# Filter and scan of a recurrent branch on PSUM banks, with another order of steps, and another start of a streamed two-block kernel

## The chip, the cores and the metric

One core of a Trainium2 chip runs the kernel; it has a matmul engine (TensorE, PE in the profile), VectorE (DVE), ScalarE (ACT), GpSimd (POOL) and SyncE (SP), an on-chip memory SBUF and the eight PSUM banks into which TensorE writes. The metric is the device time of one launch in microseconds, lower is better. TensorE's granted clock has two levels, 2.4 GHz (1.00 in the profile) and 1.2 GHz (0.50).

## The reference

Two blocks in float32, on 512 tokens of width 1024 and, in the first block, 256 context tokens more (768 in all). Cut to what matters here:

```python
# first block: adaLN, then a mixer whose projections pass a short filter
sh1, sc1, g1, sh2, sc2, g2 = adaln(c, ada_w[layer], ada_b[layer])
h_lat = modulate(rms_norm(x, norm_mix_g[layer]), sh1, sc1)
# second block, two layers: the recurrent branch of its mixer, 4 heads of 256
xc = causal_depthwise_conv(x_r, rc_w, RNN_CONV_K) + rc_b          # 4 taps
gates = jax.nn.sigmoid(einsum('bshi,ghij->gbshj', xh, rg_w) + rg_b)
log_a = -LRU_C * gate_rec * jax.nn.softplus(-a_param)
a = jnp.exp(log_a)
mult = jnp.sqrt(-jnp.expm1(2.0 * log_a))                           # 1 at the first token
h = associative_scan(a, x * gate_in * mult)                        # h_t = a_t h_(t-1) + b_t
y_b = (h * jax.nn.gelu(y_r)) @ w_out_rnn
g_a, g_b = jnp.split(jax.nn.sigmoid(g_logits + b_merge), 2, axis=-1)
out = (g_a * y_a + g_b * y_b) @ w_o
```

## The kernel before, in words

**The stream.** All projections but adaLN's read weights as 543 chunks of 512 KB (8 tiles of 128x128). SP loads a chunk into one of two `raw` slots; ACT makes its high part `w_hi` (L987), POOL the rest `w_lo` (L415), each in four slots; TensorE makes 16 products with the high part (L442, L443, with the two parts of the activations) and 8 with the low part (L447). `chunk` (L432) is one such step. ACT makes a high part when it reaches `done()` in its own stream, so it does so between its other steps.

**The start.** Six parts of adaLN are summed up on TensorE from 48 rows of `ada_w` (`part_chunk`, L451); the 16 rows of parts 0 and 1 come in eight 1 MB loads on SP (`load_first`). A part lies in one bank as four strips of two rows, at partitions 0, 32, 64 and 96: DVE copies the bank to `arow` (`part_rows`, L1393), TensorE turns it with eight small float32 products (`turn_part`, L466), DVE adds the bias. x comes in eight loads of 384 KB on ACT's queue. ACT squares x (L1006), DVE adds the squares (L1391), two products with ones (L480, L481) sum them over the partitions; then the root, the scaling of x (L1409), parts 0 and 1, and h1, one k-tile at a time (L1428). TensorE's order: 10 rows of `ada_w`, the two ones products, `turn_part(0)`, 6 rows, `turn_part(1)`; then the projections as "items" of one chunk for 768 or 512 tokens. Item 0 (k of head 0) waits for h1 k by k, item 1 (rk) follows, item 2 (k of head 1) begins when ACT has read item 0's banks (L1044, L1045). DVE filters item 0 (L1448, L1450); products with ones for its norm stand behind item 2 on TensorE (L523, L524). Parts 2 to 5 are turned behind items 6, 13, 20 and 27.

**The recurrent branch**, two times (one per layer). TensorE makes per head h two chunks of x_r (into banks 0 and 1), the gate chunk of head h-1 (`head_gates`, banks 4 to 7) and two chunks of y_r (banks 2 and 3): five chunks a head. ACT copies x_r from the bank to a padded row in SBUF (`rows`, L1281); DVE filters it there (L1883, three times L1885) to xc, whose high part ACT makes (L1286) and whose low part DVE (L1893). After the gate chunk ACT takes four sigmoids (L1304, L1305) and exp and tanh (L1311, L1312); DVE multiplies (L1900), squares (L1903), combines (L1906); ACT takes the root (L1318); DVE sets the first token to 1 (L1912), multiplies (L1913), scans (L1914), multiplies by gelu(y_r) (L1917) and makes the low part (L1923), ACT the high part (L1291). All of head h-1 lies inside the period of head h, in both engines' order. `head_gates(h)` on TensorE waits for head h-1's sigmoids (`s_sig`).

**Behind it** come for m = 0 to 7 `conv_gates(m)` (three chunks: the convolution branch's product and two gates, in banks 0, 1, 3 for even m, 4, 5, 7 for odd m) and `rnn_product(m)` (bank 2 or 6). TensorE's order: `conv_gates(0)` (which waits for the last x_r copy and for gelu of y_r of head 3, L1298), `head_gates(3)`, a wait for its sigmoids, `conv_gates(1)`, `conv_gates(2)`, then the products. ACT takes the gates' sigmoids in pairs (`gate_pair`, L1333), DVE multiplies the first by the bank (`gated_conv`, L1860).

DVE's ops that add a product to an SBUF row elsewhere are L1787 and L1827.

## Time and profile before

| | |
|---|---|
| median of 3 runs | 3640.2 us (3639.19 to 3641.14) |
| profiled execution, its own time | 3641.35 us |
| its span | 3639.5 us, 45258 instructions |
| granted TensorE clock, mean | 0.973 |
| busy: PE, PEld, DVE, ACT, POOL | 94%, 78%, 39%, 38%, 36% |
| chain that ended last | PE 61%, issue 27%, POOL 5%, DVE 4%, ACT 3% |

The sum of a prediction for one execution goes against 3641.35 us, of which 1.85 us lie around the span. A row of the timeline groups like instructions that follow each other closely; the bracket at its end is the engine's idle time before it and what ended it.

### The profile page before, as it was taken

How to read it: one execution, taken by the hardware profiler on the slowest of the kernel's cores; microseconds unless marked ns; L12 is line 12 of the kernel's file. 1: busy time of each engine (PE TensorE's matmuls, PEld its weight loads, DVE VectorE, ACT ScalarE, POOL GpSimd, SP SyncE). 2: the span in 40 equal slices, each digit the busy share in tenths (PEclk: the TensorE clock that was granted, in tenths of full speed). 3: DMA queues.
4: the chain of work that ended last, by engine and by line, in shares of the span. 5: the costliest groups of instructions: out<-in, count | busy, mean ns of one | idle time of the engine just before them, and what ended most of it. 6: DMA issues, size and time to landing. Idle time of an engine off the chain costs nothing.

```text
span 3639.5 us, 45258 instructions
## 1 busy us (share of the span) xinstructions
PE 3425.6 (94%) x16376; PEld 2829.5 (78%) x16376; DVE 1404.4 (39%) x1696; ACT 1369.6 (38%) x1812; POOL 1310.6 (36%) x547
## 2 busy tenths in 40 slices
PE   5999899899998999899799999989998989989997
PEld 4777799778887888788687888778887867878885
DVE  5753555532204220656415321142207473262214
ACT  3434344544414441325523443244323264234423
POOL 1232000044443444344344444334443433434443
PEclk7999999999999999999899999999999999999998
DMA  6342000122222222232232223222222222223222
GB/s 236 115 140 80 2 1 1 36 92 98 98 94 80 98 98 95 79 99 87 81 99 87 87 97 98 82 92 97 94 98 81 98 76 93 93 71 108 93 98 87
DMA packets 89456, 322.08 MB, mean 88 GB/s; under 512 B 9712, under 2 KB 10096, under 8 KB 89200
## 3 DMA queue, kind: packets, MB, share of 16 engines
q1 hardware_dynamic: 87136, 315.07, 25.9%
q10 hardware_dynamic: 2192, 5.24, 0.4%
q8 instruction: 88, 1.44, 0.2%
q14 instruction: 40, 0.33, 0.0%
HBM read 318.18 MB, written 2.10 MB: 88 GB/s over the span
## 4 chain that ended last, share of the span: by engine, by line
PE 61%; issue 27%; POOL 5%; DVE 4%; ACT 3%; POOLq 0%; DMA 0%; DVEq 0%; ACTq 0%; SPq 0%
PE ps L442 14%; PE ps L443 14%; PE ps L447 14%; POOL w_lo L415 5%; PE ps L762 5%; PE ps L839 4%; PE ps L835 4%; PE ps L836 4%; DVE mt L1906 1%; PE ps L862 1%; PE ps L861 1%; PE ps L860 1%; ACT w_hi L987 1%; DVE tmp L1885 0%; DVE X L1756 0%
## 5 line engine op out<-in xcount | busy, mean ns | idle before, releaser
L415 POOL TENSOR_TENSOR w_lo<-raw,w_hi 128x1024 fp32r<-128x1024 f32 x543 | 1310.4, 2414 | 2309.8 <-ACT w_hi L987 2309.6
L987 ACT ACTIVATE w_hi<-raw 128x1024 fp32r<-128x1024 f32 x543 | 574.9, 1060 | 1557.8 <-PE ps L447 972.4
L442 PE MATMUL ps<-acts,w_hi 128*128 128x512 f32 x2848 | 1113.5, 391 | 48.9 <-ACT tmp L1298 32.9
L443 PE MATMUL ps<-acts,w_hi 128*128 128x512 f32 x2848 | 1111.9, 390 | 0.0
L447 PE MATMUL ps<-acts,w_lo 128*128 128x512 f32 x2848 | 703.3, 389 | 0.0
L442 PEld LDWEIGHTS ps<-acts,w_hi 128*128 128x128 f32 x2848 | 537.0, 189 | 165.5 <-ACT w_hi L987 42.9
L443 PEld LDWEIGHTS ps<-acts,w_hi 128*128 128x128 f32 x2848 | 537.1, 189 | 111.6
L447 PEld LDWEIGHTS ps<-acts,w_lo 128*128 128x128 f32 x2848 | 534.5, 188 | 111.0
L1787 DVE TENSOR_TENSOR tmp<-tmp,ps 128x512 f32<-128x512 f32 x110 | 75.6, 687 | 684.8 <-PE ps L447 626.6
L835 PE MATMUL ps<-acts,w_hi 128*128 (+1 forms) x760 | 295.6, 389 | 0.0
L836 PE MATMUL ps<-acts,w_hi 128*128 (+1 forms) x760 | 295.6, 389 | 0.0
L1790 DVE TENSOR_TENSOR acts<-tmp,acts 128x512 f32 x110 | 237.7, 2161 | 149.1 <-ACT acts L1251 149.1
L762 PE MATMUL ps<-acts,w_hi 128*128 128x512 f32 x640 | 183.7, 420 | 60.8 <-ACT acts L1241 44.9
L762 PEld LDWEIGHTS ps<-acts,w_hi 128*128 128x128 f32 x640 | 130.6, 206 | 97.4 <-issue 48.1
L839 PE MATMUL ps<-acts,w_lo 128*128 (+1 forms) x760 | 187.7, 389 | 0.0
L1827 DVE SCALAR_TENSOR_TENSOR X<-ps,X 128x512 f32<-128x512 f32 x32 | 22.1, 692 | 417.4 <-PE ps L862 414.7
L839 PEld LDWEIGHTS ps<-acts,w_lo 128*128 128x128 f32 x760 | 142.6, 188 | 29.6
L835 PEld LDWEIGHTS ps<-acts,w_hi 128*128 128x128 f32 x760 | 142.7, 188 | 29.6
L836 PEld LDWEIGHTS ps<-acts,w_hi 128*128 128x128 f32 x760 | 142.6, 188 | 29.6
L987 ACT ACT_TABLE_LOAD x55 | 70.6, 1283 | 204.1 <-PE ps L447 175.8
L442 PE MATMUL ps<-h,w_hi 128*128 128x512 f32 x336 | 128.5, 394 | 8.9 <-DVE h L1428 8.4
L443 PE MATMUL ps<-h,w_hi 128*128 128x512 f32 x336 | 118.8, 367 | 0.0
(366 smaller groups left out, 3420.0 us busy)
## 6 DMA issues: line engine op xcount, KB each, us to landing
raw<-stream SPq DMA_DIRECT2D x543, 512.0 KB, 3.3
ada_behind<-ada SPq DMA_DIRECT2D x32, 512.0 KB, 3.5
ada_first<-ada SPq DMA_DIRECT2D x8, 1024.0 KB, 15.8
xin<-x_in ACTq DMA_DIRECT2D x8, 384.0 KB, 10.8
X<-x_in ACTq DMA_DIRECT2D x1, 2048.0 KB, 8.6
...
```

The costliest lines, as they stand in the source:

```text
L415: nc.gpsimd.tensor_tensor(w_lo[:, slot, :, :], raw[:, slot % RAW, :, :], f32(w_hi[:, slot, :, :]), ALU.subtract).then_inc(s_lo, 1)
L442: mm(o, w_hi[:, s, k, :], xh, start=start, stop=False, skip_group_check=True)
L443: mm(o, w_hi[:, s, k, :], xl, start=False, stop=False, skip_group_check=True)
L447: last = mm(o, w_lo[:, s, k, :], xh, start=False, stop=stop, skip_group_check=True)
L762: part = lambda w, x: (lambda j, k: mm(ps[banks[j]][:, :], w[:, slots[j], k, :], pair(first + k)[x], start=(k == 0 and w is w_hi and x == ...
L835: mm(ps[m][:, :], w_hi[:, s, m, :], hh, start=a, stop=False, skip_group_check=True)
L836: mm(ps[m][:, :], w_hi[:, s, m, :], hl, start=False, stop=False, skip_group_check=True)
L839: last = mm(ps[m][:, :], w_lo[:, s, m, :], hh, start=False, stop=False, skip_group_check=True)
L860: mm(ps[m][:, :], w_hi[:, s, m, :], hh, start=False, stop=False, skip_group_check=True)
L987: A(w_hi[:, s, :, :], raw[:, s % RAW, :, :], ACT.Copy).then_inc(s_hi, 1)
L1787: TT(tmp[1][:, :], tmp[0][:, :], ps[2 * j + 1][:, :], ALU.mult).then_inc(s_prod, 1)
L1790: TT(acts[:, bass.ds(i * 2 + (8 + j), 1), 1, :], tmp[1][:, :], f32(acts[:, bass.ds(i * 2 + (8 + j), 1), 0, :]), ALU.subtract).then_inc(s_h ...
```

## The change

- x is loaded in four pieces of two k-tiles: two on SP ahead of the first load of `ada_w`, two on ACT.
- `arow` is two rows of 1024: DVE fills it with four copies in place of one, and TensorE turns a part with eight transposes against a 2x2 identity in place of eight products.
- TensorE's start: 8 rows of `ada_w`, the ones products, 4 rows, `turn_part(0)`, 4 rows, `turn_part(1)`. Items 0 and 1 are made together, k by k, as h1 comes (`first_items`).
- Recurrent branch: DVE filters x_r right from the bank; ACT's row copies and `s_xr` are gone, TensorE waits for the filter to be over before it writes x_r of the next head. The first sigmoid stays in banks 4, 5; tanh goes to banks 6, 7; the combined term and its root to 4, 5; the scan's result to 6, 7. The squares move from DVE to ACT.
- A head's steps on DVE are spread over two periods: `gate_inputs` of head h-1 and `scans`, `low_h` of head h-2 stand in head h's period, and the two rows' filters are apart. ACT takes the roots at the start of the next period. `head_gates(h)` on TensorE waits for `s_hg`, the scans of h-1.
- `conv_gates` 0, 1 and 2 all use banks 0, 1, 3; 1 and 2 wait until the gates and the gated product of the one before are read. ACT's gates are single steps between its others.

```diff
+        merge_bank = lambda m: 0 if m < 3 else 4 * (m % 2)
+        forerunner = lambda m: m - 1 if m < 3 else m - 2
...
+            for k in (0, 2):
+                sp.dma_start(xin[:, k:k + 2, :], x_in[:, k:k + 2, :]).then_inc(s_xin, 16)
             load_first(0)
...
             def turn_part(part, bank):
                 pe.wait_ge(s_arow, part + 1)
                 for m in range(KT):
-                    q, o = m // 2, m % 2 * P
-                    last = mm(ps[bank][:, 2 * m:2 * m + 2], arow[:, o:o + P], ident[:, 32 * q:32 * q + 2],
-                              start=True, stop=True)
+                    last = nc.tensor.transpose(ps[bank][:, 2 * m:2 * m + 2], arow[0:2, m * P:(m + 1) * P],
+                                               ident[0:2, 0:2])
                 last.then_inc(s_acol, 1)
 
             pe.wait_ge(s_csil, 1)
-            for n in range(2 * FIRST):
+            for n in range(KT):
...
+            for n in range(KT, KT + 4):
+                part_chunk(n, n // KT)
             turn_part(0, 6)
-            for n in range(2 * FIRST, 2 * KT):
+            for n in range(KT + 4, 2 * KT):
                 part_chunk(n, n // KT)
             turn_part(1, 7)
+
+            def first_items():
+                slots = [(slot[0] + i) % SLOTS for i in range(2)]
+                slot[0] += 2
+                for k in range(TILES):
+                    pe.wait_ge(s_h1, k + 1)
+                    for i, s in enumerate(slots):
+                        if k == 0:
+                            pe.wait_ge(s_hi, n_hi.up())
+                        for o, xh, xl in ((ps[2 * i][:, :], h1[:, k, 0, CTX:TOK], h1[:, k, 1, CTX:TOK]),
+                                          (ps[2 * i + 1][:, 0:CTX], h1[:, k, 0, 0:CTX], h1[:, k, 1, 0:CTX])):
+                            mm(o, w_hi[:, s, k, :], xh, start=(k == 0), stop=False, skip_group_check=True)
+                            mm(o, w_hi[:, s, k, :], xl, start=False, stop=False, skip_group_check=True)
+                    for i, s in enumerate(slots):
+                        if k == 0:
+                            pe.wait_ge(s_lo, n_lo.up())
+                        for o, xh in ((ps[2 * i][:, :], h1[:, k, 0, CTX:TOK]),
+                                      (ps[2 * i + 1][:, 0:CTX], h1[:, k, 0, 0:CTX])):
+                            last = mm(o, w_lo[:, s, k, :], xh, start=False, stop=(k == KT - 1),
+                                      skip_group_check=True)
+                        if k == KT - 1:
+                            last.then_inc(s_done, 1)
...
-                        pe.wait_ge(s_sig, n_mix["half"].up())
+                        pe.wait_ge(s_hg, n_mix["half"].up(2))
...
+                            pe.wait_ge(s_xcf, n_mix["row"].up())
                         chunk(x_outs(ps[j]))
...
                 def conv_gates(m):
-                    b = 4 * (m % 2)
-                    if m >= 2:
-                        pe.wait_ge(s_merge, merges.now + gated(m - 2))
-                        pe.wait_ge(s_mg, n_mix["mg"].up(2))
+                    b = merge_bank(m)
+                    if m and m != 3:
+                        pe.wait_ge(s_merge, merges.now + gated(forerunner(m)))
+                        pe.wait_ge(s_mg, n_mix["mg"].now + 2 * forerunner(m) + 2)
...
-                pe.wait_ge(s_sig, n_mix["half"].up())
+                n_mix["half"].up(2)
                 conv_gates(1)
...
-            for k in range(KT):
-                act.dma_start(xin[:, k, :], x_in[:, k, :]).then_inc(s_xin, 16)
+            for k in (4, 6):
+                act.dma_start(xin[:, k:k + 2, :], x_in[:, k:k + 2, :]).then_inc(s_xin, 16)
...
-                def rows(h, j):
-                    done()
-                    A(mt[j][:, 3:LAT + 3], ps[j][:, :], ACT.Copy).then_inc(s_xr, 1)
-
-                def split_rows(h):
-                    for j in range(2):
-                        act.wait_ge(s_xcf, xcf.up())
-                        A(acts[:, xcp(h, j), 0, :], xcb(h, j), ACT.Copy).then_inc(s_xch, 1)
+                def split_row(h, j):
+                    act.wait_ge(s_xcf, xcf.up())
+                    A(acts[:, xcp(h, j), 0, :], xcb(h, j), ACT.Copy).then_inc(s_xch, 1)
...
-                        A(mt[6 + j][:, 0:LAT], ps[4 + j][:, :], ACT.Sigmoid, bias=lay[:, L_RGB + f:L_RGB + f + 1])
+                        A(ps[4 + j][:, :], ps[4 + j][:, :], ACT.Sigmoid, bias=lay[:, L_RGB + f:L_RGB + f + 1])
...
+                        last = A(ps[6 + j][:, :], mt[8 + j][:, 0:LAT], ACT.Tanh, scale=lay[:, L_N8 + f:L_N8 + f + 1])
+                    last.then_inc(s_ath, 1)
+                    act.wait_ge(s_ath, ath.up())
+                    for j in range(2):
+                        last = A(mt[12 + j][:, 0:LAT], mt[10 + j][:, 0:LAT], ACT.Square)
+                    last.then_inc(s_ath, 1)
+                    ath.up()
...
+                        A(ps[4 + j][:, :], ps[4 + j][:, :], ACT.Sqrt).then_inc(s_root, 1)
 
                 for h in range(H):
-                    rows(h, 0)
+                    if h > 1:
+                        roots()
+                    done()
+                    split_row(h, 0)
                     if h > 1:
                         split_h(h - 2)
-                    rows(h, 1)
-                    split_rows(h)
+                    done()
+                    split_row(h, 1)
                     if h:
                         head_gates(h - 1)
                     gelus(h)
-                    if h:
-                        roots()
                 yb.up(4)
 
...
+                def gate(m, g):
+                    done()
+                    A(gates[m % 3][g], ps[merge_bank(m) + 1 + 2 * g][:, :], ACT.Sigmoid,
+                      bias=lay[:, L_BM + g * KT + m:L_BM + g * KT + m + 1]).then_inc(s_mg, 1)
+
+                roots()
                 done()
-                gate_pair(0)
+                gate(0, 0)
                 split_h(H - 2)
+                gate(0, 1)
                 head_gates(H - 1)
                 done()
+                gate(1, 0)
                 roots()
-                gate_pair(1)
+                gate(1, 1)
                 done()
                 split_h(H - 1)
-                gate_pair(2)
+                gate(2, 0)
+                gate(2, 1)
...
                 dve.wait_ge(s_ada, KT * (part + 1))
-                CP(arow[:, :], ps[bank][:, 0:2 * P]).then_inc(s_arow, 1)
+                for q in range(4):
+                    last = CP(arow[0:2, 2 * P * q:2 * P * (q + 1)], ps[bank][32 * q:32 * q + 2, 0:2 * P])
+                last.then_inc(s_arow, 1)
...
+                def filter_row(h, j):
+                    f, y = 2 * h + j, xcb(h, j)
+                    dve.wait_ge(s_done, done.now + (5 * h + j if h else j + 1))
+                    link(TS(y, ps[j][:, :], par(L_RC + 3 * KT + f), par(L_RCB + f), ALU.mult, ALU.add))
+                    for s in (1, 2, 3):
+                        last = STT(y[:, s:LAT], ps[j][:, 0:LAT - s], par(L_RC + KT * (3 - s) + f), y[:, s:LAT],
+                                   ALU.mult, ALU.add)
+                        if s < 3:
+                            link(last)
+                    last.then_inc(s_xcf, 1)
+                    dve.wait_ge(s_xcf, xcf.up())
+                    dve.wait_ge(s_xch, xch.up())
+                    TT(acts[:, xcp(h, j), 1, :], y, f32(acts[:, xcp(h, j), 0, :]), ALU.subtract).then_inc(s_xc, 1)
+
+                def gate_inputs(h):
+                    dve.wait_ge(s_sig, sig.up())
+                    for j in range(2):
+                        last = TT(mt[6 + j][:, 0:LAT], ps[4 + j][:, :], xcb(h, j), ALU.mult)
+                    link(last)
+                    dve.wait_ge(s_ath, ath.up(2))
+                    for j in range(2):
+                        last = STT(ps[4 + j][:, :], mt[12 + j][:, 0:LAT], 1.0, ps[6 + j][:, :], ALU.add, ALU.mult)
+                    last.then_inc(s_m2, 1)
+                    m2.up()
+
+                def scans(h):
+                    dve.wait_ge(s_root, root.up(2))
+                    for j in range(2):
+                        last = V.memset(ps[4 + j][:, 0:1], 1.0)
+                    link(last)
+                    for j in range(2):
+                        last = TT(mt[6 + j][:, 0:LAT], ps[4 + j][:, :], mt[6 + j][:, 0:LAT], ALU.mult)
+                    link(last)
+                    for j in range(2):
+                        last = V.tensor_tensor_scan(ps[6 + j][:, :], mt[10 + j][:, 0:LAT], mt[6 + j][:, 0:LAT], 0.0,
+                                                    ALU.mult, ALU.add)
+                    link(last)
+                    dve.wait_ge(s_gelu, gelu.up(2))
+                    for j in range(2):
+                        TT(geb(h, j), ps[6 + j][:, :], geb(h, j), ALU.mult).then_inc(s_hg, 1)
+                    hg.up(2)
+
+                def low_h(h):
+                    dve.wait_ge(s_hg, hg.now)
+                    for j in range(2):
+                        p = 16 + 2 * h + j
+                        dve.wait_ge(s_ybh, ybh.up())
+                        TT(acts[:, p, 1, :], geb(h, j), f32(acts[:, p, 0, :]), ALU.subtract).then_inc(s_yb, 1)
+
+                for h in range(H):
+                    if h > 1:
+                        scans(h - 2)
+                    filter_row(h, 0)
+                    if h > 1:
+                        low_h(h - 2)
+                    filter_row(h, 1)
                     if h:
...
+                        gate_inputs(h - 1)
+                scans(H - 2)
+                low_h(H - 2)
+                gated_conv(0)
+                gate_inputs(H - 1)
                 gated_conv(1)
+                scans(H - 1)
+                low_h(H - 1)
                 gated_conv(2)
```

The start of item 0 on TensorE, before (ps0 and ps1 are item 0's banks, the 512 and the 256 tokens; the rows then repeat for each k):

```order
L442 MATMUL ps0<-h1_49,w_hi_81 128x512 [waits h1,hi]
L443 MATMUL ps0<-h1_49,w_hi_81 128x512
L442 MATMUL ps1<-h1_49,w_hi_81 128x256
L443 MATMUL ps1<-h1_49,w_hi_81 128x256
L442 MATMUL ps0<-h1_49,w_hi_81 128x512 [waits h1]
...
```

and with the change:

```order
L497 MATMUL ps0<-h1_49,w_hi_81 128x512 [waits hi,h1]
L498 MATMUL ps0<-h1_49,w_hi_81 128x512
L497 MATMUL ps1<-h1_49,w_hi_81 128x256
L498 MATMUL ps1<-h1_49,w_hi_81 128x256
L497 MATMUL ps2<-h1_49,w_hi_81 128x512 [waits hi]
L498 MATMUL ps2<-h1_49,w_hi_81 128x512
L497 MATMUL ps3<-h1_49,w_hi_81 128x256
L498 MATMUL ps3<-h1_49,w_hi_81 128x256
L504 MATMUL ps0<-h1_49,w_lo_82 128x512 [waits lo]
L504 MATMUL ps1<-h1_49,w_lo_82 128x256
L504 MATMUL ps2<-h1_49,w_lo_82 128x512 [waits lo]
L504 MATMUL ps3<-h1_49,w_lo_82 128x256
```

Item 1's products (ps2, ps3) now stand between those of item 0, and the low parts of both (`w_lo`, `waits lo`) in each k in place of behind all of them.

DVE in a head, before, from the squares on (order prints the scan as SCALAR_TENSOR_TENSOR; mt are SBUF rows):

```order
L1903 TENSOR_TENSOR mt8_144<-mt10_146 128x512 [waits ath]
L1903 TENSOR_TENSOR mt9_145<-mt11_147 128x512
...
L1906 SCALAR_TENSOR_TENSOR mt8_144<-mt8_144,mt12_148 128x512 [waits dve]
L1906 SCALAR_TENSOR_TENSOR mt9_145<-mt9_145,mt13_149 128x512
L1912 MEMSET mt8_144 128x1 [waits root,m2]
...
L1913 TENSOR_TENSOR mt6_142<-mt6_142,mt8_144 128x512 [waits dve]
...
L1914 SCALAR_TENSOR_TENSOR mt12_148<-mt10_146,mt6_142 128x512 [waits dve]
...
L1917 TENSOR_TENSOR mt4_140<-mt12_148,mt4_140 128x512 [waits gelu,dve]
L1912 MEMSET mt9_145 128x1 [waits root]
...
L1913 TENSOR_TENSOR mt7_143<-mt7_143,mt9_145 128x512 [waits dve]
```

and with the change, from the roots' wait on, where a new head's filter follows:

```order
L1934 MEMSET ps4 128x1 [waits root]
L1934 MEMSET ps5 128x1
...
L1937 TENSOR_TENSOR mt6_142<-ps4,mt6_142 128x512 [waits dve]
L1937 TENSOR_TENSOR mt7_143<-ps5,mt7_143 128x512
...
L1940 SCALAR_TENSOR_TENSOR ps6<-mt10_146,mt6_142 128x512 [waits dve]
L1940 SCALAR_TENSOR_TENSOR ps7<-mt11_147,mt7_143 128x512
...
L1945 TENSOR_TENSOR mt4_140<-ps6,mt4_140 128x512 [waits gelu,dve]
L1945 TENSOR_TENSOR mt5_141<-ps7,mt5_141 128x512
...
L1909 TENSOR_SCALAR mt2_138<-ps0,lay_87 128x512 [waits done]
...
L1918 TENSOR_TENSOR acts_50<-mt2_138,acts_50 128x512 [waits xch,xcf]
L1953 TENSOR_TENSOR acts_50<-mt4_140,acts_50 128x512 [waits ybh,hg]
L1953 TENSOR_TENSOR acts_50<-mt5_141,acts_50 128x512 [waits ybh]
```

The combination that the roots wait for has left this place (it stands in the period before), the roots', scans' and combinations' rows lie in ps4 to ps7, and a filtered row (L1909 to L1918) stands between a scan and its low part (L1953).

TensorE between `head_gates(3)` and `conv_gates(1)`, before:

```order
L447 MATMUL ps<-acts,w_lo 128x512 [waits lo]
L447 MATMUL ps<-acts,w_lo 128x512 x7
L947 REGISTER_ALU
L437 REGISTER_ALU [waits sig]
L442 MATMUL ps<-acts,w_hi 128x512 [waits hi]
L443 MATMUL ps<-acts,w_hi 128x512
```

and with the change (the waits are those of `gated` and of the gates):

```order
L446 MATMUL ps<-acts,w_lo 128x512 [waits lo]
L446 MATMUL ps<-acts,w_lo 128x512 x7
L958 ISA
L959 REGISTER_ALU [waits merge]
L438 REGISTER_ALU [waits mg]
L441 MATMUL ps<-acts,w_hi 128x512 [waits hi]
L442 MATMUL ps<-acts,w_hi 128x512
```

`conv_gates(1)` waited there for the sigmoids of head 3, and now for what ACT and DVE read of `conv_gates(0)`; the same two waits stand ahead of `conv_gates(2)`, as before.

## Rows read from the trace of the kernel before

**Rows 1.** The page: busy time, share of the span and instructions of each engine.

```profile
PE 3425.6 (94%) x16376; PEld 2829.5 (78%) x16376; DVE 1404.4 (39%) x1696; ACT 1369.6 (38%) x1812; POOL 1310.6 (36%) x547
```

**Rows 2.** Windows of the start: stretch, engines' busy us (count), TensorE clock, DMA share, GB/s.

```profile
20.00:30.00 10.00, 5.96 (x51) 2.64 (x52) 7.61 (x9) 7.53 (x9) 0.00 (x0) 0.88 1.03 407
```

**Rows 3.** Timeline, 19 to 55 us: start, duration, engine, line, operation [idle before <-releaser].

```profile
19.71 2.31 ACT L1006 ACTIVATE big<-xin 128x768 f32<-128x768 f32 x3 [12.94 <-DMA xin<-x_in]
...
22.61 1.77 PE L462 MATMUL ps<-ada_first,cond 128*32 128x256 f32 x16 [0.64 <-DMA ada_first<-ada]
...
25.18 1.07 PE L462 MATMUL ps<-ada_first,cond 128*32 128x256 f32 x16 [0.80 <-DMA ada_first<-ada]
...
28.81 1.19 PE L480 MATMUL ps<-big,ones 128*128 128x256 f32 x2 [2.56 <-DVE big L1391]
...
46.72 0.42 DVE L1395 COPY arow<-ps 128x256 f32<-128x256 f32 x1
...
47.20 3.58 PE L470 MATMUL ps<-ident,arow 128*128 128x2 f32 x16 [8.16 <-DVE arow L1395]
...
54.26 0.76 PE L442 MATMUL ps<-h,w_hi 128*128 128x512 f32 x1 [3.48 <-DVE h L1428]
```

**Rows 4.** Timeline, around the second item: TensorE, ACT, VectorE, POOL.

```profile
75.65 0.50 PE L442 MATMUL ps<-h,w_hi 128*128 128x512 f32 x1
...
84.82 0.50 PE L442 MATMUL ps<-h,w_hi 128*128 128x512 f32 x1
...
76.36 0.58 ACT L1045 ACTIVATE big<-ps 128x512 f32<-128x512 f32 x1
...
76.97 1.73 DVE L1448 TENSOR_SCALAR big<-big,prm 128x772 f32<-128x772 f32 x1 [7.07 <-ACT big L1045]
78.74 4.20 DVE L1450 SCALAR_TENSOR_TENSOR big<-big,prm,big 128x772 f32<-128x772 f32 x4
...
75.89 2.39 POOL L415 TENSOR_TENSOR w_lo<-raw,w_hi 128x1024 fp32r<-128x1024 f32 x1 [12.08 <-ACT w_hi L987]
```

**Rows 5.** Timeline, TensorE: a part is turned, twice, and six transposes.

```profile
135.44 1.84 PE L470 MATMUL ps<-ident,arow 128*128 128x2 f32 x16
...
201.28 3.34 PE L470 MATMUL ps<-ident,arow 128*128 128x2 f32 x16 [2.36 <-DVE arow L1395]
...
316.95 0.54 PE L535 MATMUL ps<-ident,big 16*128 16x16 f32 x6 [1.89 <-ACT big L1056]
```

**Rows 6.** Timeline, VectorE, first layer: heads 1 and 2 come to their scans.

```profile
1723.93 0.06 DVE L1912 MEMSET mt<- 128x1 f32 x1 [0.80 <-ACT mt L1318]
...
1724.75 1.22 DVE L1914 TENSOR_TENSOR_SCAN mt<-mt,mt 128x512 f32<-128x512 f32 x1
...
1757.35 0.06 DVE L1912 MEMSET mt<- 128x1 f32 x1 [0.80 <-ACT mt L1318]
```

**Rows 7.** Timeline, ACT, first layer: the last row split, then the roots of that head.

```profile
1740.52 0.63 ACT L1286 ACTIVATE acts<-tmp 128x512 fp32r<-128x512 f32 x1 [2.19 <-DVE tmp L1885]
...
1756.58 1.15 ACT L1318 ACTIVATE mt<-mt 128x512 f32<-128x512 f32 x2 [1.29 <-DVE mt L1906]
```

**Rows 8.** Groups by line and form: count | busy us, mean ns | idle before <-releaser.

```profile
L1787 DVE TENSOR_TENSOR tmp<-tmp,ps 128x512 f32<-128x512 f32 x110 | 75.6, 687 | 684.8 <-PE ps L447 626.6 <-ACT tmp L1248 58.1
...
L1914 DVE TENSOR_TENSOR_SCAN mt<-mt,mt 128x512 f32<-128x512 f32 x16 | 25.8, 1613 | 0.5
...
L1827 DVE SCALAR_TENSOR_TENSOR X<-ps,X 128x512 f32<-128x512 f32 x32 | 22.1, 692 | 417.4 <-PE ps L862 414.7
L1885 DVE SCALAR_TENSOR_TENSOR mt<-mt,lay,mt 128x512 f32<-128x512 f32 x24 | 22.1, 920 | 0.8
```

**Rows 9.** Timeline, TensorE, first layer, around its two pauses.

```profile
1754.23 0.79 PE L442 MATMUL ps<-acts,w_hi 128*128 128x512 f32 x1 [16.48 <-ACT tmp L1298]
...
1759.74 1.98 PE L447 MATMUL ps<-acts,w_lo 128*128 128x512 f32 x8
...
1781.57 0.49 PE L442 MATMUL ps<-acts,w_hi 128*128 128x512 f32 x1 [3.53 <-ACT mt L1305]
```

96 lines of the change are left out of this document (19 added, 77 removed).

## The prediction

> **What bounds the kernel now.** I read the page first: TensorE is busy 3425.6 us of the span, 94% [rows 1], and most of it are chunks of 24 passes of 512 columns; eight take 1.98, of which the last 0.39 lies over the next instruction [rows 9], so a pass adds 0.227 and a chunk 5.44 at full clock. So a change to VectorE or ACT is worth only what TensorE stops waiting. The table of windows shows where that is: in the start, where the DMA engines are full (407 GB/s, share 1.03) and TensorE has little to do [rows 2], and at one place of each layer. The timeline of the start says which wait ends last there: squares begin when x has landed (19.71), TensorE takes their sums at 28.81, the first product on h1 starts at 54.26 [rows 3]. Of the recurrent branch the timeline of TensorE shows no gap until 1754.23, where it has stood for 16.48 us, and again 3.53 us at 1781.57 [rows 9]; the second layer shows the same two gaps. Behind the first the low part of the chunk starts 5.51 us after the high part began, whose 16 passes make 3.63 at full clock, so 1.9 is lost to a clock that has fallen to 1.2 GHz during the gap [rows 9]; behind the second 1.7 in the same way. A layer therefore loses 16.5 + 1.9 + 3.5 + 1.7 = 23.6 us. The first gap is there because ACT and VectorE need 1757.35 - 1723.93 = 33.4 us for a head [rows 6], TensorE 5 x 5.44 = 27.2, so that after three heads TensorE's lead in free banks is used up.
>
> **The change, step by step.** Gains are taken from 3641.35, the profiled execution's own time, which stands 1.15 above the median. A measurement of this kernel can tell 0.2%, or 7.3 us, from no change.
>
> *x ahead of the weights.* x is 3.1 MB, 7.7 us at 407 GB/s [rows 2]; it lands near 11 in place of 19.7 [rows 3]. Squares and sums take 28.81 - 19.71 = 9.1 and would be over at 20. But the ones products now stand behind 8 rows of `ada_w`, four loads, and a load takes 25.18 - 22.61 = 2.57 when the queue is full [rows 3]: 11 + 4 x 2.6 = 21.4, and the last load's products 1.9, give 23.4. Everything behind hangs on the sums, so **5.4** is gained. If the loads come as unevenly as in the first 20 us, the gain is 2; more than 5.4 is not to be had behind four loads.
>
> *Turning a part.* Part 1 takes TensorE 3.58 us for 16 passes at the low clock [rows 3]; eight transposes take half, and six small ones took 0.54 [rows 5]. It saves 1.75. Three more copies like the 0.42 one [rows 3] stand in front, which overlap in part: 1.0. Net **0.75**. For parts 2 to 5 the passes cost 1.84 at full clock [rows 5], half of it saved four times is 3.7; but where VectorE comes late, as at 201.28 [rows 5], the copies' 1.0 lies on TensorE's path. I take two of four: **2**, bounds 0 and 3.7.
>
> *Items 0 and 1 together.* From the first product to item 2 before: 84.82 - 54.26 = 30.6 [rows 3, 4], since item 0 waits for every h1(k), takes 75.65 - 54.26 = 21.4 for products worth 8.2 (24 passes of 0.227 and 24 of half that), and item 1 only follows. Now each h1(k) brings work for both, 2 us, which fills that waiting: 16.4 in all, and 2.0 for the low clock at its beginning. Item 2 must wait till ACT has read item 0's banks, which end now at the same time as item 1's: the split of a chunk and the read. Before, that read ended at 76.94, 1.3 behind the beginning of item 1 [rows 4], ahead of which lie 16 passes on `ada_w` of 1.07 [rows 3]; so 2.3. Together 20.7, or 9.9 saved. Part of it is given back: the two filter steps of item 0 take 1.73 + 4.20 [rows 4], they now meet POOL's two low parts of 2.39 [rows 4] in a row, and behind come a table load, exp and square on ACT; that is 11.5 us against the 8.8 that cover it (item 2's 8.2 and eight passes on `ada_w`). TensorE waits 2.7 ahead of item 0's norm, and loses 1.5 in clock behind it. Net **5.7**, between 0 (the pieces behind item 0 are bound by VectorE anyway) and 9.9.
>
> *The recurrent branch's cycle.* Both orders remain serial in one place: VectorE's scans, filter 0, filter 1, then ACT's split of the last row, sigmoids, exp and tanh, gelus and roots, then VectorE's scans of the next. Between the last split and the end of the roots ACT takes 1757.73 - 1740.52 = 17.2 now, 15.9 without the 1.29 it waits for VectorE [rows 7]. Squares on ACT add 2 x 0.6: 17.1. VectorE's part is then two scans 2.4 at 1.22 [rows 6], four products 2.7 at 0.69 [rows 8], two filters of four ops, each 0.69 [rows 8] with little between, 2.9 each, the split that the first low part waits for 0.8, three low parts 1.9, and 0.2 to wake: 13.8. Sum 31 in place of 33.4. What speaks against it is the row of the scan: 1.22 where it ran alone, but 1.61 in the mean of 16 [rows 8], so some ran at twice or more, while products with a bank in them took 0.687 in the mean of 110 [rows 8]. The scan keeps two SBUF inputs, and if POOL holds them in each cycle for the better part of one low part (2.39 [rows 4]), 2.3 come back: 33.3. So the cycle gains between 0.1 and 2.4; I take 1.35, a little over the middle, since the scans start at another point of POOL's beat in each cycle. TensorE's end of the branch lags by two such cycles: **2.7 per layer, 5.4 in all**, bounds 0.4 and 9.6. *Where the wait goes:* TensorE now waits for scans at `head_gates(1)` and `head_gates(2)`, for gelu at `conv_gates(0)`, some 3 to 5 us each in place of one gap of 16.5. The 3.5 us gap at 1781.57 [rows 9] stays in other form: `conv_gates(2)` waits for the gates of the one before, a split 1.0, a table load and a sigmoid, 3.6. `conv_gates(1)` has `head_gates(3)` of 5.44 us to cover the same wait, and costs nothing. The copies of rows removed (ACT, 0.58 each) were off this path. Writes to a bank by ACT or VectorE are in no row; the nearest is that reading one costs 0.69 against 0.92 (held) for the same op between SBUF rows [rows 8], so I price them at nothing; bounds -0.1 and +0.6 us each.
>
> Of the filter the rows say 0.69 from the bank against 0.92 from SBUF in the mean [rows 8]. The Trainium skill, "VectorE: DVE Perf Modes", section "Rules for kernel authors", says that elementwise work on a product may read PSUM at the slow rate or should be copied to SBUF first "if you'll do many ops": four ops read the row here, so the page leans to the code before, by which this term would be nothing or a small loss.
>
> **The sum**: 5.4 + 0.75 + 2 + 5.7 + 5.4 = 19.25, so 3622.1 for a profiled execution and 3621.0 for the median. By the bounds it is 3611 to 3634.
>
> **The rivals.**
> *R1, the cycle falls under TensorE's 27.2.* If ACT's part of a head overlapped VectorE's more than the two orders let it, the 16.5 gap and its clock would vanish: 2 x 18.4 = 36.8 in place of 5.4, so 3590. For it: each engine alone has less than 20 us of work per head. Against: `split_row(h,1)` stands ahead of the sigmoids on ACT, and the roots ahead of the scans.
> *R2, POOL holds VectorE, and the gain is given back.* Both scans are held in every cycle, so that the branch brings 0.4; and the filters of the items, two SBUF rows each, are held in the same way behind a start that comes earlier, so that 5.7 is 0 and of the 5.4 for x about 3 are left: 3641.35 - 3 - 0.75 - 1 - 0.4 = 3636.2, a median of 3635.0, within 7.3 of before. For it: the scan's mean [rows 8]. Against: item 2 and its neighbours leave VectorE idle for 7.07 us ahead of a filter [rows 4]. The Trainium skill, "SBUF — State Buffer", section "Who interferes with whom", states the rule: a VectorE instruction with two SBUF inputs contends with a POOL instruction that reads SBUF. By that rule, with which the scan's and the bank's rows agree, the cycle stands at 33.3 wherever a scan meets a low part.
> *R3, slower: writes to a bank cost more.* Ten ops per cycle (sigmoid, tanh, combination, root, scan, each twice) write to banks now. At +0.6 us each a cycle is 6 longer; three cycles, two layers make 36: 3622 + 36 = 3658, median 3657. It passes zero at 19.25/60 = 0.32 us a write, and shows as slower from 0.44. For it: no row shows such a write. Against: reads of a bank cost nothing.
> *R4, x is not earlier,* because four pieces on two queues share the engines with the first loads: 2 to 5 us less; inside the forecast's range.
>
> **How the numbers follow.** Forecast 0.78 (3611 to 3634, nearly all of it over 7.3 us faster), R1 and its halfway forms 0.07, R2 0.10, R3 0.05. The range leaves out R1's far end and R3: 3604 to 3636. Faster by over 0.2% 0.84, within 0.2% 0.10, slower 0.06.
>
> **What would show it.** Right: the ones products near 23.4; the first product on h1 near 48; item 2 some 21 us behind it, with a wait of 2 to 3 us ahead of item 0's norm; the memsets of the scans 31 to 33 us apart; waits on VectorE's gelu product at the gate chunks of heads 1 and 2, and none on the sigmoids. Wrong: a scan or root row over 1.5 us with no POOL work beside it (R3), head distances of 27.2 (R1) or 33.3 and more (R2), ones products at 28 (R4). If the memsets are 31 apart and TensorE still ends the branch as late as before, the step that turns cycles into TensorE's time is wrong.

## The result, and the profile after

The changed kernel takes 3617.35 us in the median of 4 runs (3615.60 to 3617.76), the kernel before beside it 3640.67 (3639.19 to 3642.07). The ratio is 0.9935, with a 95% interval of 0.9918 to 0.9952: 23.3 us faster, against 19.7 forecast (3621.0), inside the range. The profiled execution took 3617.55, its span is 3615.7; the clock's mean rose from 0.973 to 0.978.

The sum came out, its parts did not. Where a place of the program lies in the two spans:

| place on TensorE | before | after | earlier by |
|---|---|---|---|
| ones products start | 28.81 | 25.60 | 3.2 |
| first product on h1 | 54.26 | 45.11 | 9.2 |
| item 2 starts | 84.82 | 66.91 | 17.9 |
| six transposes behind the items | 316.95 | 296.93 | 20.0 |
| start of the stretch ahead of layer 0 (a 9 us wait on silu) | 1501.80 | 1481.09 | 20.7 |
| the 0.55 us wait behind layer 0's mixer | 1942.43 | 1919.47 | 23.0 |
| the same of layer 1 | 3191.68 | 3168.07 | 23.6 |

So in these two executions the start brought 20.7, where the prediction's terms give 13.85, and the branch 2.25 and 0.7 us, where they give 5.4. The timeline of the start, changed kernel (start, duration, engine, line, operation, idle before and what ended it):

```profile
11.80 2.31 ACT L1032 ACTIVATE big<-xin 128x768 f32<-128x768 f32 x3 [6.12 <-DMA xin<-x_in]
...
25.60 0.70 PE L478 MATMUL ps<-big,ones 128*128 128x256 f32 x2 [1.29 <-DMA cst<-consts]
26.13 1.02 PE L479 MATMUL ps<-big,ones 128*128 128x512 f32 x2
...
30.57 7.04 DVE L1441 TENSOR_TENSOR xin<-xin,big 128x768 f32<-128x768 f32 x8 [4.40 <-ACT big L1036]
...
36.71 5.40 POOL L418 TENSOR_TENSOR w_lo<-raw,w_hi 128x1024 fp32r<-128x1024 f32 x2 [36.26 <-ACT w_hi L1013]
...
45.11 0.79 PE L497 MATMUL ps<-h,w_hi 128*128 128x512 f32 x1 [4.47 <-DVE h L1460]
...
66.91 0.50 PE L441 MATMUL ps<-h,w_hi 128*128 128x512 f32 x1 [0.50 <-ACT big L1071]
...
76.91 0.70 PE L549 MATMUL ps<-big,ones 128*128 128x256 f32 x2 [0.76 <-ACT big L1100]
```

x has landed at 11.8 (the first square begins), 7.9 earlier than in [rows 3]. The scaling of x (L1441) takes 7.04 us and is over at 37.6; POOL's first low part starts at 36.7. In the kernel before it looked like this:

```profile
35.13 11.35 DVE L1409 TENSOR_TENSOR xin<-xin,big 128x768 f32<-128x768 f32 x8 [6.13 <-ACT big L1010]
...
37.24 5.82 POOL L415 TENSOR_TENSOR w_lo<-raw,w_hi 128x1024 fp32r<-128x1024 f32 x2 [36.79 <-ACT w_hi L987]
```

The same eight products of two SBUF rows each took 11.35 us and lay over POOL's first two low parts. Being 4.6 us earlier, they are 4.3 us shorter.

This is not a fixed gain of the change. Eight of the kernels that follow in this document (counting the changed one) have the same start, line by line. In four profiled executions (changed kernel, scan_roots, split_waits, start_split) the ones products ran at full clock, the scaling began at 30.6 to 30.7, took 7.04, and the first product stood at 45.1 to 45.2. In the other four (start_only, scan_bank, roots_early, squares_dve) they ran at the low clock, the scaling began at 31.9 to 32.0, took 11.33, and the first product stood at 49.6 to 49.7. At the wait on silu ahead of layer 0 the first four lie between 1474.86 and 1481.09, the others between 1480.21 and 1482.68. So what the start brings, read from one execution, is uncertain by a few us.

The two layers' branch on TensorE, changed kernel, layer 0:

```profile
1675.82 0.57 PE L441 MATMUL ps<-acts,w_hi 128*128 128x512 f32 x1 [2.22 <-DVE mt L1945]
...
1708.97 0.49 PE L441 MATMUL ps<-acts,w_hi 128*128 128x512 f32 x1 [4.06 <-DVE tmp L1945]
...
1732.54 0.79 PE L441 MATMUL ps<-acts,w_hi 128*128 128x512 f32 x1 [5.34 <-ACT tmp L1319]
...
1776.53 0.49 PE L441 MATMUL ps<-acts,w_hi 128*128 128x512 f32 x1 [3.30 <-ACT sg L1362]
```

In place of [rows 9], 16.48 and 3.53, stand four pauses, 14.9 us together. VectorE in a head cycle, and the low part that POOL makes beside the pair of scans:

```profile
1661.81 1.29 DVE L1927 SCALAR_TENSOR_TENSOR ps<-mt,ps 128x512 f32<-128x512 f32 x2 [3.82 <-ACT mt L1337]
1668.45 0.07 DVE L1934 MEMSET ps<- 128x1 f32 x2 [5.35 <-ACT ps L1344]
...
1669.88 4.49 DVE L1940 TENSOR_TENSOR_SCAN ps<-mt,mt 128x512 f32<-128x512 f32 x2
1674.40 1.29 DVE L1945 TENSOR_TENSOR mt<-ps,mt 128x512 f32<-128x512 f32 x2
...
1701.62 0.07 DVE L1934 MEMSET ps<- 128x1 f32 x2 [5.34 <-ACT ps L1344]
...
1669.77 2.39 POOL L418 TENSOR_TENSOR w_lo<-raw,w_hi 128x1024 fp32r<-128x1024 f32 x1 [1.79 <-ACT w_hi L1013]
```

The memsets stand 33.17 us apart, and 33.14 the next time, against 33.4 [rows 6]: the cycle hardly got shorter. Two scans took 4.49 us while a low part of POOL ran beside them, and 4.47 in the next head; the pair of head 2 (1736.18), with none beside it, 2.35. Groups of the changed kernel, by line and form:

```profile
L1940 DVE TENSOR_TENSOR_SCAN ps<-mt,mt 128x512 f32<-128x512 f32 x16 | 31.0, 1984 | 0.3
...
L1326 ACT ACTIVATE mt<-ps,lay 128x512 f32<-128x512 f32 x16 | 11.0, 689 | 0.0
...
L1325 ACT ACTIVATE ps<-ps,lay 128x512 f32<-128x512 f32 x16 | 10.5, 658 | 0.1
L1927 DVE SCALAR_TENSOR_TENSOR ps<-mt,ps 128x512 f32<-128x512 f32 x16 | 10.4, 693 | 30.5 <-ACT mt L1337 30.5
```

and of the kernel before, the combination between SBUF rows (which L1927 answers to):

```profile
L1906 DVE SCALAR_TENSOR_TENSOR mt<-mt,mt 128x512 f32<-128x512 f32 x16 | 35.9, 2282 | 0.3
```

Sigmoids into a bank take 658 ns, into SBUF 689; the combination, in a bank, 693 in place of 2282. The scan's mean rose from 1613 [rows 8] to 1984: more of them lie beside a low part of POOL.

The windows of the branch (stretch, engines' busy us, the granted clock, DMA share, GB/s):

```profile
1710.00:1720.00 10.00, 10.00 (x38) 8.07 (x37) 7.39 (x11) 4.93 (x7) 3.07 (x2) 0.83 0.16 54
1730.00:1740.00 10.00, 7.46 (x23) 5.96 (x24) 5.00 (x8) 4.64 (x7) 3.74 (x2) 0.66 0.34 105
1770.00:1780.00 10.00, 6.70 (x30) 5.26 (x29) 7.23 (x9) 6.26 (x8) 3.70 (x2) 1.00 0.48 154
```

Behind the pauses at 1708.97 and 1732.54 the clock fell, behind the one at 1776.53 it did not.

### The profile page after: what moved, and what is told of

The parts are those of the page before. It is cut to its first block, busy times and chain, and to the rows that moved or that the text cites. A ratio compares the mean times of both kernels' runs of the same rounds, so it can differ in the third digit from the quotient of the medians.

```text
span 3615.7 us, 45138 instructions
## 1 busy us (share of the span) xinstructions
PE 3416.7 (94%) x16328; PEld 2818.8 (78%) x16328; DVE 1348.3 (37%) x1694; ACT 1372.9 (38%) x1814; POOL 1307.9 (36%) x547
## 4 chain that ended last, share of the span: by engine, by line
PE 62%; issue 27%; POOL 5%; ACT 3%; DVE 2%; POOLq 0%; DMA 0%; DVEq 0%; ACTq 0%; SPq 0%
PE ps L441 15%; PE ps L442 15%; PE ps L446 14%; POOL w_lo L418 5%; PE ps L788 5%; PE ps L865 4%; PE ps L861 4%; PE ps L862 4%; PE ps L888 1%; PE ps L887 1%; PE ps L886 1%; ACT w_hi L1013 1%; DVE X L1788 0%; DVE ps L1940 0%; DVE tmp L1911 0%
## 5 line engine op out<-in xcount | busy, mean ns | idle before, releaser
L441 PE MATMUL ps<-h,w_hi 128*128 128x512 f32 (+1 forms) x304 | 115.1, 390 | 0.5 <-ACT big L1071 0.5
L442 PE MATMUL ps<-h,w_hi 128*128 128x512 f32 (+1 forms) x304 | 106.5, 363 | 0.0
## 6 DMA issues: line engine op xcount, KB each, us to landing
ada_first<-ada SPq DMA_DIRECT2D x8, 1024.0 KB, 13.2
```

Source lines behind the costliest of these rows:

```text
L441: mm(o, w_hi[:, s, k, :], xh, start=start, stop=False, skip_group_check=True)
L442: mm(o, w_hi[:, s, k, :], xl, start=False, stop=False, skip_group_check=True)
```

## The experiments

Medians; each run had the kernel before beside it (medians 3639.6 to 3641.7), and the changed kernel's 3617.35 is the mark for edits to it. The changed kernel itself was not run again beside them, and the kernel before moved by 2 us between these sittings, so a difference of under 3 us from the mark is not told from none by the medians. "L0" is the time from the wait on silu ahead of layer 0's mixer to the 0.55 us wait behind it in the profiled execution: 440.6 in the kernel before, 438.4 in the changed one; L1 is the same of layer 1, 440.8 and 440.0.

### The parts alone

**start_only**: the changed kernel's start, the branch of before.

> The whole new start (x ahead of the weights, the turning of the parts, the order of TensorE's start, items 0 and 1 together) with the recurrent branch of before. Theory A, read from the two traces (item 2 starts 17.9 us earlier, the stretch at 440 us lies 20.8 earlier): the start alone brings 20.8, so 3640.7 - 20.8 = 3619.9. Theory B, the terms of the prediction (5.4 + 0.75 + 5.7 + 2 = 13.85), the rest of the measured gain coming from the branch or from an interplay: 3626.8.

Measured 3621.62, ratio 0.9950 (0.9933 to 0.9967): 18.8 gained, nearer to Theory A's 20.8 than to Theory B. Its profiled execution shows the other form of the start:

```profile
25.63 1.22 PE L477 MATMUL ps<-big,ones 128*128 128x256 f32 x2 [2.02 <-DMA cst<-consts]
26.64 1.91 PE L478 MATMUL ps<-big,ones 128*128 128x512 f32 x2
...
31.98 11.33 DVE L1436 TENSOR_TENSOR xin<-xin,big 128x768 f32<-128x768 f32 x8 [6.52 <-ACT big L1035]
...
49.72 0.79 PE L496 MATMUL ps<-h,w_hi 128*128 128x512 f32 x1 [3.39 <-DVE h L1455]
```

The ones products start at 25.63 as in the changed kernel, but at the low clock (1.22 and 1.91 against 0.70 and 1.02, with the same instructions). The scaling begins at 31.98 in place of 30.57, meets POOL, and takes 11.33. So 1.4 us lost to the clock put the scaling's end 5.7 later, of which 4.6 are left at the first product (49.72). Of these 2.3 are left at the transposes and 0.9 at layer 0's stretch; what took up the rest was not looked into.

**branch_only**: the start of before, the changed branch.

> The whole new recurrent branch with the start of before. Theory A, from the traces (layer 0 gains 2.3 us, layer 1 0.8, because POOL holds both scans of a head, 4.5 us a pair, and the head cycle is 33.2): 3.1 gained, 3637.6. Theory B, the prediction's 2.7 per layer: 3635.3. If the branch needed the new start to pay (another phase of the streams against each other), it gives anything between 3632 and 3641.

Measured 3639.31, ratio 0.9996 (0.9987 to 1.0006): 1.1 gained, not to be told from none. L0 is 438.4 as in the changed kernel, L1 442.9, 2.8 more than the changed kernel's with 1.4 less of pauses, so it was the clock behind the pauses that made it longer. The same branch stands in early_sums below, where L1 is 442.8 too: two of three executions gained nothing in the two layers together, the changed kernel's own 3.0. The branch's part of the change is worth 0 to 3 us, decided by the clock behind the pauses; the two parts add up (18.8 + 1.1) to 3.4 less than both together.

**x_only** (two x loads of two k-tiles on SP ahead of `load_first(0)`, two on ACT, in place of eight on ACT).

> Only the x loads are moved ahead of all weights; TensorE still makes ten rows of ada_w ahead of the ones products. Theory A: x lands near 11 and the squares are summed near 21, but the ones products start behind the fifth load, near 27 in place of 28.8; the scaling of x begins 2 us earlier and still meets one or two of POOL's low parts (it took 11.35 us in before, 7.04 in the changed kernel, where POOL had not begun): 9 to 11 us. Together 3 to 5 us gained, 3636 to 3638. Theory B, the scaling's 4.3 us come with x alone, since the first weights land no earlier: 6 gained, 3634.5.

Measured 3634.78 over 10 runs (3630.48 to 3638.99), ratio 0.9987 (0.9978 to 0.9997). The profiled execution, 3638.99, is the slowest of them, and shows the first product at 51.83, 2.4 earlier, and the scaling at 11.33 as before: Theory A's mechanism in this execution. Five of the ten lie at 3633.5 or less; whether the scaling was short in them, as Theory B has it, no trace shows. The median's 5.7 is near Theory B's 6, and by the interval the gain lies anywhere between 1 and 8.

**pair_only** (`first_items` in place of two chunks).

> Only items 0 and 1 together, k by k; everything else of before. Theory A, from the changed kernel's trace (first product to item 2 takes 21.8 us in place of 30.6, and the wait ahead of item 0's norm is 0.8): 8 us gained, 3632.7. Theory B, the prediction's term with 2.7 of wait and 1.5 of clock given back: 5.7 gained, 3635.0.

Measured 3630.65, ratio 0.9974 (0.9964 to 0.9984): 9.8 gained, 1.8 more than Theory A. First product to item 2 took 76.14 - 54.36 = 21.8 in place of 30.6, and the wait ahead of item 0's norm was 0.69. Items 0 and 1 together are the largest part of the change.

### The head cycle

**scan_bank**

```diff
-                        last = TT(mt[6 + j][:, 0:LAT], ps[4 + j][:, :], mt[6 + j][:, 0:LAT], ALU.mult)
+                        last = TT(ps[4 + j][:, :], ps[4 + j][:, :], mt[6 + j][:, 0:LAT], ALU.mult)
...
-                    last = V.tensor_tensor_scan(ps[6 + j][:, :], mt[10 + j][:, 0:LAT], mt[6 + j][:, 0:LAT], 0.0,
+                    last = V.tensor_tensor_scan(ps[6 + j][:, :], mt[10 + j][:, 0:LAT], ps[4 + j][:, :], 0.0,
```

> The changed kernel, but the product ahead of the scan is written in place to banks 4 and 5 and the scan reads it there: one SBUF input in place of two, nothing else. Theory A (POOL holds the scans because they have two SBUF inputs): the pair of scans takes 2.4 in place of 4.5 in each cycle, the distance of the memsets falls from 33.2 to 31.0, TensorE waits 4.4 less per layer and loses less clock: 8 to 10 us gained on the changed kernel, 3608 to 3609.5. Theory B (a scan that writes to a bank is slow by itself, or is held through its output or the other row): the pair stays at 4.5, 3617.4. Theory C (the scan of a bank's row is slower than that of an SBUF row by some 0.3): 2.9, 5 us gained.

```profile
1668.92 0.07 DVE L1934 MEMSET ps<- 128x1 f32 x2 [5.35 <-ACT ps L1344]
...
1670.35 2.34 DVE L1940 TENSOR_TENSOR_SCAN ps<-mt,ps 128x512 f32<-128x512 f32 x2
...
1699.96 0.07 DVE L1934 MEMSET ps<- 128x1 f32 x2 [5.34 <-ACT ps L1344]
...
1670.15 2.40 POOL L418 TENSOR_TENSOR w_lo<-raw,w_hi 128x1024 fp32r<-128x1024 f32 x1 [1.71 <-ACT w_hi L1013]
```

Measured 3614.93. The mechanism of Theory A is shown: POOL's low part lies over the pair as it did in the changed kernel, the pair takes 2.34, and the memsets are 31.04 apart, the 31 of the prediction for scans that are not held. Its price is not: 2.4 us in place of 8 to 10, within what the medians can't tell from none. Pauses fell from 14.9 to 11.3 and from 15.3 to 11.2, but L0 only from 438.4 to 437.2, L1 from 440.0 to 437.2. Behind the last pause (3.30 in both kernels) the clock now falls:

```profile
1770.00:1780.00 10.00, 6.84 (x18) 5.42 (x19) 4.97 (x8) 3.00 (x3) 2.35 (x1) 0.66 0.21 77
```

against 1.00 in the same stretch of the changed kernel. The time that TensorE no longer stands still it partly spends at the low clock.

**roots_early** (`roots()` behind `head_gates(h - 1)`, ahead of `gelus(h)`).

> The changed kernel, but ACT takes the roots of a head right behind its squares, ahead of the gelus, in place of behind them. Theory A (ACT and VectorE are serial in one loop, and everything on ACT between the last sigmoid and the roots is in it): two gelus, two splits and a table load, 4.4 us, leave the loop, against a wait of 1 to 1.5 for the combination on VectorE; the cycle falls from 33.2 to about 30, TensorE waits 6 us less per layer: 3605 to 3608. Theory B (TensorE then waits for gelu instead, since banks 2 and 3 come free 3 us later): the waits move to the gelu, and the gain is under 3 us: 3615 or more.

Measured 3615.71: 1.6 gained, Theory B. The cycle fell from 33.2 to 30.8 (scans at 1667.22 and 1698.03), though the scan pair, now at another point beside POOL's low parts, took 6.3 us in place of 4.5. The pause at conv_gates(0), on gelu, grew from 5.3 to 6.7, as Theory B says; the one at `head_gates(1)` is gone, and all pauses of a layer fell to 13.2.

**scan_roots**: both.

> The last two edits together. Theory A: the cycle is 33.2 - 2.2 - 3.2 = 27.8, within 1 us of TensorE's 27.2, so the waits at the gate chunks vanish and the one at conv_gates(0) shrinks to under 2 us; what is left per layer is the wait for the gates at conv_gates(2) and its clock, 5 us: 15 us gained per layer, up to 30, 3587 to 3592. Theory B (another step becomes the bound, such as the splits on ACT that wait for chunks, or y_r's banks): no more than the better one of the two alone, 3605 or more.

Measured 3610.37; cycle 30.3, not 27.8. The low parts of x and h, with two SBUF rows, are held instead (3.48 us for two in place of 1.29). The waits at the gate chunks are gone, as Theory A says, but all of them came back in one place: 12.3 us at conv_gates(0), on the gelu of bank 3. The time lies in Theory B's range (3605 or more), but the 7.0 gained are more than the better of the two alone brought (2.4), which Theory B excluded.

**squares_dve**: squares back on VectorE, behind the tanh.

> The changed kernel with the squares back on VectorE, between its waits. In the loop two squares on ACT (1.15 us, and the wake between) are replaced by two on VectorE (1.29, two SBUF rows each, so POOL can hold them by up to 2.1) behind the tanh. Theory A (the move off VectorE was worth only the hold): the cycle is 33.2 to 35.3, 3617.4 to 3626. Theory B (ACT is the engine that binds, less on it is a gain): 3613 to 3616.

Measured 3611.41: 5.9 faster than the changed kernel, Theory B and 1.6 below its range. The scans are 32.0 apart (1667.78, 1699.81) in place of 33.2: the 1.15 us on ACT are gone and VectorE's squares cost the loop nothing. By this run the move of the squares to ACT, a part of the change, was a loss. L0 fell to 434.9, L1 only to 439.3, with 0.6 less of pauses than L0.

### What TensorE waits for

The four runs leave one picture. Their cycles differ (31.0, 30.8, 30.3, 32.0), but the two layers together took 874.2 to 874.6 us in the profiled execution of each, 4 less than the changed kernel's 878.4. TensorE stands 11 to 16 us a layer, 6.9 to 15.7 of it at two waits that lie ahead of three chunks each, `conv_gates(0)` and `conv_gates(2)`.

**split_waits**

```diff
-                    if m and m != 3:
-                        pe.wait_ge(s_merge, merges.now + gated(forerunner(m)))
-                        pe.wait_ge(s_mg, n_mix["mg"].now + 2 * forerunner(m) + 2)
+                    behind = m and m != 3
+                    if m == 0:
+                        pe.wait_ge(s_xcf, n_mix["row"].now - 1)
+                    if behind:
+                        pe.wait_ge(s_merge, merges.now + gated(forerunner(m)))
                     chunk(lambda k: [(ps[b][:, :], *pair(8 + k), k == 0, k == KT - 1)])
+                    if m == 0:
+                        pe.wait_ge(s_xcf, n_mix["row"].now)
+                    if behind:
+                        pe.wait_ge(s_mg, n_mix["mg"].now + 2 * forerunner(m) + 1)
                     chunk(x_outs(ps[b + 1]))
+                    if m == 0:
+                        pe.wait_ge(s_gelu, n_mix["gate"].now)
+                    if behind:
+                        pe.wait_ge(s_mg, n_mix["mg"].now + 2 * forerunner(m) + 2)
                     chunk(x_outs(ps[b + 3]))
...
-                pe.wait_ge(s_xcf, n_mix["row"].now)
-                pe.wait_ge(s_gelu, n_mix["gate"].now)
```

> The changed kernel, but each of conv_gates' three chunks waits only for the bank that it writes: conv_gates(0) no longer waits ahead of its first chunk for the gelu of bank 3, which only its third chunk writes, and conv_gates(2) no longer ahead of its first chunk for the gate of bank 3. Nothing else. Theory A (these two pauses, 5.3 and 3.3 us, and the low clock behind them, are what is left of the branch's cost, and 10.9 us of work stand ready to cover them): 8.6 us of pauses and 2 to 4 of clock go per layer, 3592 to 3598. Theory B (the chain of ACT and VectorE moves the pause to the next place, head_gates(3) on the scans or conv_gates(1) on the gates): the sum of the pauses per layer falls by under 4 us, 3608 or more.

Measured 3595.23, ratio 0.9880 (0.9864 to 0.9896): 22 us less than the changed kernel, 22.2 of it in the two layers by the traces. Theory A. Only the pauses at the two gate chunks are left in layer 0:

```profile
1674.67 0.49 PE L441 MATMUL ps<-acts,w_hi 128*128 128x512 f32 x1 [2.31 <-DVE mt L1953]
...
1707.93 0.79 PE L441 MATMUL ps<-acts,w_hi 128*128 128x512 f32 x1 [4.17 <-DVE tmp L1953]
```

L0 is 428.7, L1 427.4. The edit moves waits at `conv_gates(0)`, `(1)` and `(2)`; how much each brought was not measured apart.

**start_split**: the new start, the branch of before, and of that edit only what concerns conv_gates(0).

> The new start with the recurrent branch of before, and in it only the wait of conv_gates(0) split: its first two chunks wait for the row copies, the third for the gelu of bank 3. Theory A (what the branch loses is a wait for one bank ahead of three chunks, whatever the head cycle): of the pause of 16.5 us 10.9 are covered, 5.6 stay, and the second pause of 3.5 stays; 21 to 26 us gained on the run of the new start alone (3621.6), 3596 to 3601, so the same edit brings as much to the old branch as to the new one, and the new branch is worth some 5 us beside it. Theory B (the edit pays only where the head cycle is short, since in the old branch head 3's gate chunk then waits for the low parts or sigmoids instead): under 12 us gained, 3610 or more.

Measured 3602.52 (3596.60 to 3604.38): 19.1 gained on start_only, nearer to Theory A. The two pauses of layer 0:

```profile
1727.32 0.79 PE L440 MATMUL ps<-acts,w_hi 128*128 128x512 f32 x1 [5.73 <-ACT tmp L1327]
...
1744.84 0.79 PE L440 MATMUL ps<-acts,w_hi 128*128 128x512 f32 x1 [4.64 <-ACT mt L1334]
```

L0 and L1 are 430.7 and 432.8, 18.3 together under start_only's. The profiled execution is the fastest of the four and also reached layer 0 7.1 us earlier than start_only's, with the same code up to there, which is chance. A wait moved by two chunks brings 19 us to the branch of before, where the rewriting of filter and scan brought 0 to 3. The new branch with its split waits is 7.3 us better (3595.23 against 3602.52), but split_waits also moved the wait at `conv_gates(2)`, which start_split did not; the changed kernel stood 3.3 us a layer there. What the new branch is worth with the same edit in both was not run.

**early_sums**: constants loaded ahead of `ada_w`, ones products behind 6 rows.

> The changed kernel, but the three loads of constants go ahead of the first rows of ada_w, and the ones products stand behind 6 rows in place of 8. Theory A (the ones products wait 1.3 us for the constants and for the fourth load, while the squares are summed up at 20.7): they start near 22 in place of 25.6, the scaling of x is over 3.6 us earlier, but the first product on h1 hangs then on the last rows of ada_w, which land at 34.35 as before, and gains 1 to 1.6: 3616 to 3616.5. Theory B (the sums alone set the first product): 3.6 gained, 3613.8.

Measured 3616.73, 0.6 less than the mark: nearer to Theory A. The ones products start at 22.33, 3.3 earlier; the first product at 44.34, only 0.8. VectorE's second set of copies (L1426) waits for the last rows of `ada_w` and begins at 36.09, 1.8 earlier, and the two small steps behind it (L1447) take 2.33 in place of 1.33, both times up to the end of POOL's second low part. The execution came to layer 0 at 1478.29, 2.8 earlier, and lost as much to the clock in layer 1 (L1 442.8 against 440.0).

**best_a**: scan_bank, roots_early, split_waits and early_sums together.

> The changed kernel with the scan on a bank's row, the roots ahead of the gelus, the split waits, and the early sums. Theory A: the loop of ACT and VectorE takes 30.3 as in the run of the two edits together, its lag of 2 x 3.1 and the wait of 12.3 at conv_gates(0) are covered by 10.9 us of chunks, 1 to 3 us of pauses are left per layer and hardly any clock: a layer costs 418 to 421 us from the one wait on silu to the other in place of 438 to 440, 3573 to 3582. Theory B (the lost clock comes back with any pause, and another wait appears): 3590 or more.

Measured 3575.46 (3573.76 to 3576.64), ratio 0.9822 (0.9806 to 0.9838): 64.7 us under the kernel before, 41.9 under the changed one. Layer 0:

```profile
1727.02 0.49 PE L441 MATMUL ps<-acts,w_hi 128*128 128x512 f32 x1 [1.44 <-ACT tmp L1327]
...
1755.09 0.49 PE L441 MATMUL ps<-acts,w_hi 128*128 128x512 f32 x1 [0.41 <-DVE sg L1897]
```

Theory A. scan_bank and roots_early together (scan_roots) were worth 7.0 and early_sums 0.6 ahead of the split waits; behind them the three are worth 19.8. By the traces the two layers gave 3.8 in scan_roots and give 16.4 here (839.7 against split_waits' 856.2).

## Why the prediction was right, and where it was not

**Where the start's 6.9 over the forecast lie.** At the first product 9.2 were gained, where 6.15 were forecast: 3.0. From there to item 2 and behind its norm 8.8 were gained and not given back, where 5.7 were forecast: 3.1. From item 2 to the transposes 2.1 against 2, and 0.7 more up to layer 0, for which there was no term.

**x ahead of the weights: 5.4 forecast.** x landed at 11.8 (forecast 11), but the ones products started at 25.60, not 23.4: the first load of `ada_w` was used at 14.46 only, and the products then waited 1.29 for the constants, of which the last load is issued behind the fifth of `ada_w`; that wait had no term. The products themselves were 1.35 us shorter at full clock, so the logarithm began at 27.19 in place of 31.75, 4.6 earlier. The term that was missing altogether is the scaling: 11.35 us was taken as fixed. The mechanism stood in R2 (POOL holds ops with two SBUF rows), and was applied to the filters and the scans, but not to the row of L1409, where 8 products take 8 x 0.88 when nothing holds them. That these 4.3 came is partly luck: four of the eight profiled executions with this start show it still at 11.33, as x_only does, where it begins 2.2 us later than in the changed kernel. It explains the first product, not the whole: start_only, with the scaling at 11.33, came to layer 0 still 19.8 us earlier than the kernel before.

**Turning: 0.75, and 2.** Eight transposes took 0.65 at full and 1.01 at half clock, against 1.84 and 3.58: better than half. The four copies took 1.71 against 0.42, 1.3 more where 1.0 was assumed, and the two small steps behind them (L1447) took 1.33 in place of 0.24, since they now lie beside POOL's second low part. So from the end of the scaling to the first product 0.3 was gained, not 0.75. Of parts 2 to 5 one waits 3.65 in place of 2.36; from item 2 to the transposes behind the items 2.1 us were gained, as forecast, but pair_only, which turns its parts as before, gained 0.9 over the same stretch: not all of it is the turning.

**Items 0 and 1: 5.7.** Of its two halves the first was right (8.8 saved, 9.9 forecast), and the second, 4.2 given back, was not: the wait ahead of item 0's norm was 0.76 in place of 2.7. The filter was held by POOL as forecast (its second step took 6.28 in place of 4.20), and the wait was short all the same. This is the mis-sized term of the start; pair_only brought 9.8.

**The cycle: 2.7 per layer.** The two bounds were both right to 0.2 us: 33.15 with held scans (changed kernel), 31.04 without (scan_bank). The choice between them was wrong: the value in the middle supposed that the scans start at another point of POOL's low parts in each cycle, but in both cycles the pair was held. The low part began 1.3 us behind the memset in one (1669.77) and 1.5 in the next (1703.09): POOL is released by ACT's high parts, and these stand between the loop's own steps, so POOL keeps pace with the loop. The Trainium skill, "SBUF — State Buffer", section "Who interferes with whom", gives the rule that a VectorE instruction with two SBUF inputs contends with a GpSimd instruction that reads SBUF, and scan_bank is its test here: one SBUF input less, 2.1 us less per cycle. The step that failed is the next one, that a shorter cycle is TensorE's time: clock losses behind the in-loop pauses were left out of the sum. With [rows 9], 440.6 less 20.0 of pauses and 3.6 of clock leaves 417.0 of work per layer (best_a: 419.3 less 1.9 of pauses); by this estimate the changed kernel lost 6.5 us to the clock in layer 0, scan_bank 8.9. Four pauses of 2 to 5 us cost more clock than one of 16.5 and one of 3.5.

**Where the wait goes** was right by place and nearly by size: 2.2 and 4.1 at the gate chunks of layer 0, 5.3 at conv_gates(0) (3 to 5 forecast for each), 3.3 at conv_gates(2) (3.6); in layer 1 they were 2.2, 5.6, 4.2 and 3.3. conv_gates(1) waited for nothing.

**The advice on copying PSUM** in the Trainium skill, "VectorE: DVE Perf Modes", section "Rules for kernel authors", holds only where nothing holds VectorE: the four ops of a filter took 0.54 + 2.33 = 2.9 from SBUF, 0.81 + 2.32 = 3.1 from the bank, and 0.54 + 4.34 = 4.9 from SBUF beside a low part of POOL. No run has the filter's source alone changed, so its worth in time is not shown.

**R1** did not come: the loop is serial, and 27.8 was not reached even in scan_roots. **R2** struck in the branch, with cycles of 33.15; in the start it struck item 0's filter, at no wait of TensorE over 0.76, and the scaling in four of the eight profiled executions. **R3** is out: no write to a bank was slower than one to SBUF (sigmoid 658 ns against 689, tanh 672 against 707, root 580 against 624, scan 1216 in scan_bank against some 1220). **R4** is out: x landed at 11.8.

That forecast and result lie only 3.7 us apart is therefore partly luck: the start brought 6.9 us more than its terms, the branch 2.4 less. The range had luck too: the terms' own lower bounds (2, 0.75, 0, 0 and 0.4) add up to 3637, not to the 3634 that the prediction names.
